# Attention value products of a hybrid decoder step: each product split over its queries onto the two column halves of the array

## The chip, the cores and the metric

The kernel runs on one core of one Trainium2 chip. The metric is the device time of one execution in microseconds (us); three runs of the kernel before gave 4284.92, 4284.16 and 4273.37 us, a median of 4284.16 us. Work is split over TensorE (matrix products; the profile shows its matmuls as PE and its weight loads as PEld), VectorE (DVE), ScalarE (ACT), GpSimd (POOL) and the queue that issues transfers (SP).

## The reference, cut to what matters

One decoder layer is computed for a prompt of 2048 tokens and for 8 samples. It has a combined input projection, two parallel head groups, an output projection, a SwiGLU network and an embedding gate. The two head groups of the prompt are:

- group A, a gated DeltaNet with 4 heads of width 128, which is a recurrence over chunks of tokens with a triangular system to solve in each chunk;
- group B, a dilated sliding-window attention with 8 heads of width 64, for three pairs of window and dilation, (128, 1), (512, 4) and (2048, 16). For each pair a block of 128 queries sees the keys of its own block and of the block before it, or, at dilation 16, where one block holds the whole strided sequence, of its own block alone.

The part that the change touches is the product of probabilities and values:

```python
s = einsum('bdnqhe,bdnkhe->bdnhqk', qb, kk) * (E ** -0.5) + b
pr = exp(s - max(s))
den = sum(pr)
o = einsum('bdnhqk,bdnkhe->bdnqhe', pr, vv) / den
```

## The kernel before

The program is a sequence of blocks that end one after the other: input projection, bias rows with the samples' recurrence, `delta_and_attention`, the merge with the samples' attention, output projection, gate and up, down projection, embedding gate. Only `delta_and_attention` (scratch names begin with `pb_`) is changed.

It loops over 16 chunks of 128 tokens. In one chunk it does the recurrence of group A for all four heads, and, laid between its steps, one unit of attention for each of the three dilations. A unit has 4 steps, a step is two heads, so that a chunk has 12 steps (`STEPS`). Step `j` goes through the engines so:

1. `score_pair` (L946) on TensorE: queries times keys, contraction over 64 rows, for steps `j` and `j + 1` in alternation on the upper and lower 64 rows of the array.
2. VectorE adds the bias (L1140) and takes the maximum (L1144).
3. ScalarE takes the exponential with its sum (L842).
4. `turn` (L961) on TensorE: transposes of the probabilities `e`, one per head and block of keys.
5. ScalarE copies them to `eT` (L834).
6. `values` (L972) on TensorE: for each of the two heads and each block of keys one product with `eT` as the stationary operand (128 keys by 128 queries) and 64 columns of `vtok` as the moving one, accumulated over the blocks of keys in the bank `OUTPUT`.
7. VectorE copies the bank to `uo` after each unit (L1150), and a transfer stores it.

The order on TensorE is written out by hand. `slot(j)` issues `unit_start` (L933, transposes of the values) where a unit begins, `score_pair(j)` for even `j`, `values(j - 2)` and `turn(j - 1)`; `chunk` puts slots 0 to 13 between the steps of group A. All operands here are f32. The profile shows each f32 matmul that is no transpose as two records, each with a weight load of its own, and a transpose as one. So `values` makes 8 pairs of weight load and matmul in the steps of the first two dilations, which have two blocks of keys, and 4 in those of the third: 8 x 8 + 4 x 4 = 80 in a chunk, 1280 in all.

Three forms of matmul stand in this stage. The attention's transposes and values and most of group A use the whole array, 128 rows by 128 columns; the scores use 64 rows by 128 columns; the triangular solve of group A (`in_halves`, L920) uses 64 rows by 64 columns, one product on the upper rows and the lower columns' counterpart on the lower rows, in alternation (`TOP` and `BOTTOM` are partitions 0 to 63 and 64 to 127). The profile prints the form as rows*columns.

Each engine takes its instructions in order, with semaphores between them. `values(j)` waits for `eT_copied` and, at the first step of a unit, for `o_copied`; its last matmul raises `pv_done`, for which ScalarE waits before it overwrites that `eT` buffer and VectorE before it copies the bank.

Of the kernel before, what the change touches and what calls it, by code (L numbers as in the profile page):

```python
# [552 lines left out]
def delta_and_attention(nc, t):  # L553
# [13 lines left out]
    with ExitStack() as ctx:  # L567
# [31 lines left out]
        vtok = [sbuf(f"pb_vtok{v}", [P, 2, AH * HD], F32) for v in range(len(DILS))]  # L599
# [4 lines left out]
        eT = sbuf("pb_eT", [P, 2, 4 * P], F32)  # L604
# [29 lines left out]
        def bank(n):  # L634
            return ps[:, n, :]

        TOP, BOTTOM = slice(0, HALF_CH), slice(HALF_CH, P)
# [13 lines left out]
        SCORES, TURNS, OUTPUT = 4, 6, 7  # L651
# [3 lines left out]
        def step_heads(j):  # L655

            first = j % 4 // 2 * 4 + j % 2
            return j // 4, (first, first + 2)
# [6 lines left out]
        def col(tile, h):  # L665
            return tile[:, h * P:(h + 1) * P]
# [233 lines left out]
        def _(pe):  # L900
# [4 lines left out]
            for c in range(NC):  # L905
                m = pe.transpose(ps[:, c // 8, c % 8 * 36:c % 8 * 36 + 36], logits[:, c * CH:(c + 1) * CH], ident[0:36, 0:36])
# [16 lines left out]
            def halves(par, j):  # L923

                return ((par, 1),) if j // 4 == 2 else ((1 - par, 0), (par, 1))
# [38 lines left out]
            def values(c, par, j):  # L964
                v, hs = step_heads(j)
                pe.wait_ge(eT_copied, c * STEPS + (j + 1))
                if j % 4 == 0:
                    pe.wait_ge(o_copied, c * UNITS + (v + 1))
                for n, h in enumerate(hs):
                    hh = slice(h * HD, (h + 1) * HD)  # L970
                    for unit, half in halves(par, j):
                        m = pe.matmul(bank(OUTPUT)[:, hh], col(eT[:, j % 2, :], 2 * n + half), vtok[v][:, unit, hh],  # L972
                                      start=j // 4 == 2 or half == 0, stop=half == 1)
                m.then_inc(pv_done, 1)

            def slot(c, par, j):
                if j % 4 == 0 and j < STEPS:
                    unit_start(c, par, j // 4)
                if j < STEPS and j % 2 == 0:
                    score_pair(c, par, j)  # L980
                if j >= 2:
                    values(c, par, j - 2)
                if 1 <= j <= STEPS:
                    turn(c, par, j - 1)
# [1859 lines left out]
```

## Time and profile before

| | |
|---|---|
| three runs | 4284.92, 4284.16, 4273.37 us; median 4284.16 us |
| profiled execution | 4278.54 us, of which the span from first to last instruction is 4276.8 us |
| mean granted TensorE clock | 0.905 of full speed |
| busy share of the span | PE 85%, PEld 81%, DVE 35%, ACT 27%, POOL 19% |
| stage of `delta_and_attention`, chunks only | from about 863 to 1812 us of the span |

The profile is one execution. A busy time counts the recorded duration of instructions; matmuls are pipelined and their recorded ends are modelled, so the distance from the start of one group of instructions to the start of the next says more of what they cost than their durations do. The granted clock is given as a share of full speed; its two levels are 1.2 and 2.4 GHz, 0.5 and 1.0 there.

### The profile page before, as it was taken

The numbers are of one execution on the slowest core, as the hardware profiler recorded it, in microseconds if no ns is written. First come the engines' busy times: TensorE is split into PE (matmuls) and PEld (weight loads), VectorE is DVE, ScalarE is ACT, GpSimd is POOL, SyncE is SP. The second block draws the span as 40 slices with busy tenths as digits, with TensorE's granted clock in tenths as the row PEclk, the third lists the DMA queues.
The fourth block names the chain that finished last, engine by engine and source line by source line (L and its number), as shares of the span: only waits on it lengthen the run. The fifth ranks groups of instructions, "written<-read, shape, count | busy, mean of one in ns | idle before, by whom it ended". The sixth has DMA issues, their size and how long they took to land. (4 is left out here: it accounts for less than half of the span.)

```text
span 4276.8 us, 58938 instructions
## 1 busy us (share of the span) xinstructions
PE 3653.6 (85%) x23914; PEld 3476.2 (81%) x23914; DVE 1489.8 (35%) x1892; ACT 1146.6 (27%) x2073; POOL 816.9 (19%) x428
## 2 busy tenths in 40 slices
PE   7998999598888888846784999999999699997786
PEld 6998998387777777745783999999999689887785
DVE  6451222255555555634386000000000133331443
ACT  4111211255544554510222101101011233331322
POOL 3001111111111111111310111110110344443222
PEclk9999999589889898975896999999999899998898
DMA  3223343422333233173343334211110545543310
GB/s 110 61 70 79 138 152 142 148 70 67 80 78 73 64 86 85 49 189 86 128 158 149 131 118 159 96 45 53 39 59 30 171 155 175 169 139 115 125 66 37
DMA packets 266019, 443.05 MB, mean 104 GB/s; under 512 B 55763, under 2 KB 209171, under 8 KB 250308
## 3 DMA queue, kind: packets, MB, share of 16 engines
q1 hardware_dynamic: 265868, 440.79, 32.5%
q8 instruction: 125, 2.05, 0.2%
q14 instruction: 26, 0.21, 0.0%
HBM read 300.13 MB, written 174.14 MB: 111 GB/s over the span
## 5 line engine op out<-in xcount | busy, mean ns | idle before, releaser
L78 PE MATMUL pd_prod<-pd_h_hi,pd_whi 128*128 128x412 f32 x1760 | 615.8, 350 | 34.1 <-DVE pd_h_lo L2258 34.1
L79 PE MATMUL pd_prod<-pd_h_hi,pd_wlo 128*128 128x412 f32 x1760 | 617.0, 351 | 0.0
L80 PE MATMUL pd_prod<-pd_h_lo,pd_whi 128*128 128x412 f32 x1760 | 616.9, 351 | 0.0
L78 PE MATMUL pa_proj<-pa_h_hi,pa_whi 128*128 128x412 f32 x1160 | 410.5, 354 | 53.1 <-DVE pa_h_lo L408 24.3
L79 PE MATMUL pa_proj<-pa_h_hi,pa_wlo 128*128 128x412 f32 x1160 | 409.5, 353 | 0.0
L80 PE MATMUL pa_proj<-pa_h_lo,pa_whi 128*128 128x412 f32 x1160 | 408.1, 352 | 0.0
L2267 DVE TENSOR_TENSOR pd_act<-pd_prod,pd_gate 128x412 f32<-128x412 f32 x110 | 64.5, 586 | 909.8 <-PE pd_prod L80 909.8
L78 PE MATMUL pe_prod<-pe_ahi,pe_whi 128*128 128x412 f32 x880 | 317.1, 360 | 72.2 <-POOL pe_wlo L2370 40.1
L78 PEld LDWEIGHTS pd_prod<-pd_h_hi,pd_whi 128*128 128x128 f32 x1760 | 331.9, 189 | 38.1 <-issue 29.8
L79 PEld LDWEIGHTS pd_prod<-pd_h_hi,pd_wlo 128*128 128x128 f32 x1760 | 332.1, 189 | 2.2
L80 PEld LDWEIGHTS pd_prod<-pd_h_lo,pd_whi 128*128 128x128 f32 x1760 | 331.7, 188 | 1.4
L2370 POOL TENSOR_TENSOR pe_wlo<-pe_w,pe_whi 128x1408 fp32r<-128x1408 f32 x80 | 261.3, 3286 | 309.5 <-ACT pe_whi L2381 309.1
L79 PE MATMUL pe_prod<-pe_ahi,pe_wlo 128*128 128x412 f32 x880 | 314.7, 358 | 0.0
L80 PE MATMUL pe_prod<-pe_alo,pe_whi 128*128 128x412 f32 x880 | 313.9, 357 | 0.0
L2194 POOL TENSOR_TENSOR pd_wlo<-pd_w,pd_whi 128x1024 fp32r<-128x1024 f32 x44 | 108.0, 2455 | 954.0 <-ACT pd_whi L2209 954.0
L78 PEld LDWEIGHTS pa_proj<-pa_h_hi,pa_whi 128*128 128x128 f32 x1160 | 220.7, 190 | 58.8 <-issue 35.6
L78 PEld LDWEIGHTS pe_prod<-pe_ahi,pe_whi 128*128 128x128 f32 x880 | 171.1, 194 | 79.0 <-POOL pe_wlo L2370 45.4
L79 PEld LDWEIGHTS pa_proj<-pa_h_hi,pa_wlo 128*128 128x128 f32 x1160 | 220.5, 190 | 1.9 <-issue 0.6
L80 PEld LDWEIGHTS pa_proj<-pa_h_lo,pa_whi 128*128 128x128 f32 x1160 | 220.3, 190 | 1.0
L842 ACT ACTIVATE pb_e<-pb_s,pb_uo 128x256 f32<-128x256 f32 (+1 forms) x384 | 176.7, 463 | 106.8 <-DVE pb_uo L1144 106.8
L972 PE MATMUL pb_ps<-pb_vtok,pb_eT 128*128 128x64 f32 x1280 | 193.1, 294 | 0.0
L972 PEld LDWEIGHTS pb_ps<-pb_vtok,pb_eT 128*128 128x128 f32 x1280 | 173.9, 207 | 22.3 <-issue 10.8
(353 smaller groups left out, 6291.4 us busy)
## 6 DMA issues: line engine op xcount, KB each, us to landing
pe_w<-in_w_down SPq DMA_DIRECT2D x80, 704.0 KB, 4.1
scratch_at<-pa_work SPq DMA_DIRECT2D x24, 1024.0 KB, 5.6
pb_qkv<-scratch_at SPq DMA_DIRECT2D x32, 768.0 KB, 7.3
scratch_a<-pd_act SPq DMA_DIRECT2D x22, 1030.0 KB, 5.3
pe_a<-scratch_a SPq DMA_DIRECT2D x5, 4532.0 KB, 21.3
pd_w<-in_w_gate_up SPq DMA_DIRECT2D x44, 512.0 KB, 5.9
out_new_cache_k<-in_cache_k SPq DMA_DIRECT2D x8, 2046.0 KB, 11.1
out_new_cache_v<-in_cache_v SPq DMA_DIRECT2D x8, 2046.0 KB, 16.3
```

The costliest lines, as they stand in the source:

```text
L78: pe.matmul(out, w_hi, a_hi, start=first, stop=False)
L79: pe.matmul(out, w_lo, a_hi, start=False, stop=False)
L80: return pe.matmul(out, w_hi, a_lo, start=False, stop=last)
L842: m = act.activation(keys_seen(e[:, j % 2, :], j)[:, n, :], keys_seen(s[:, j % 2, :], j)[:, n, :], ACT.Exp, bias=uo[v][:, nm:nm + 1], accu ...
L972: m = pe.matmul(bank(OUTPUT)[:, hh], col(eT[:, j % 2, :], 2 * n + half), vtok[v][:, unit, hh], start=j // 4 == 2 or half == 0, stop=half == 1)
L2194: pool.tensor_tensor(w_lo[:, par, :], w_raw[:, par, :], w_hi[:, par, :].bitcast(F32), ALU.subtract).then_inc(w_lo_done, 1)
L2267: dve.tensor_tensor(act_row[:, cols], prod_ps[:, b, 0:TB], gate[:, cols], ALU.mult).then_inc(acts_done, 1)
L2370: pool.tensor_tensor(w_lo[:, q, :], w_raw[:, q % 2, :], w_hi[:, q, :].bitcast(F32), ALU.subtract).then_inc(w_lo_done, 1)
```

## The change

In `values`, each product of 128 queries becomes two products of 64 queries each: the first half of the columns of `eT` gives partitions 0 to 63 of the output bank, the second half gives partitions 64 to 127. Both use the same moving operand. The products of the two halves are issued in alternation, for each head and block of keys. The flags `start` and `stop` stay as they were, and so does the one semaphore at the end.

```diff
                     for unit, half in halves(par, j):
-                        m = pe.matmul(bank(OUTPUT)[:, hh], col(eT[:, j % 2, :], 2 * n + half), vtok[v][:, unit, hh],
-                                      start=j // 4 == 2 or half == 0, stop=half == 1)
+                        for queries in (TOP, BOTTOM):
+                            m = pe.matmul(bank(OUTPUT)[queries, hh], col(eT[:, j % 2, :], 2 * n + half)[:, queries],
+                                          vtok[v][:, unit, hh], start=j // 4 == 2 or half == 0, stop=half == 1)
                 m.then_inc(pv_done, 1)
```

## Rows read from the trace of the kernel before

**Rows 1.** The page, busy time, share of the span and instructions of TensorE.
```profile
PE 3653.6 (85%) x23914; PEld 3476.2 (81%) x23914; DVE 1489.8 (35%) x1892; ACT 1146.6 (27%) x2073; POOL 816.9 (19%) x428
```

**Rows 2.** Busy time by stretch, with granted clock (PEclk): the stage and two chunks' lengths.
```profile
core 0: us, PE busy (x) PEld busy (x) DVE busy (x) ACT busy (x) POOL busy (x), PEclk, DMA share, GB/s
863.00:1812.00 949.00, 826.75 (x9422) 732.99 (x9420) 538.94 (x933) 482.93 (x1329) 159.17 (x172) 0.89 0.28 72
...
1043.00:1102.00 59.00, 50.18 (x531) 44.07 (x527) 29.84 (x51) 25.66 (x72) 9.06 (x10) 0.80 0.26 65
...
1751.00:1810.00 59.00, 50.47 (x621) 44.39 (x620) 36.91 (x64) 34.33 (x95) 9.22 (x10) 1.00 0.13 37
```

**Rows 3.** Groups of instructions by line in the stage, TensorE's matmuls.
```profile
L972 PE MATMUL pb_ps<-pb_vtok,pb_eT 128*128 128x64 f32 x1280 | 193.1, 294 | 0.0
```

**Rows 4.** Timeline of TensorE's matmuls: start, length, line, form, count [idle before].
```profile
1037.97 1.10 PE L972 MATMUL pb_ps<-pb_vtok,pb_eT 128*128 128x64 f32 x8
1038.91 0.60 PE L961 MATMUL pb_ps<-pb_const,pb_e 128*128 128x128 f32 x4
1039.35 1.06 PE L1022 MATMUL pb_ps<-pb_knT 128*128 128x128 f32 x8
1040.25 1.06 PE L1027 MATMUL pb_ps<-pb_qnT,pb_knT 128*128 128x128 f32 x8
1041.14 1.00 PE L972 MATMUL pb_ps<-pb_vtok,pb_eT 128*128 128x64 f32 x8
1041.98 0.61 PE L961 MATMUL pb_ps<-pb_const,pb_e 128*128 128x128 f32 x4
...
1049.77 0.68 PE L920 MATMUL pb_ps<-pb_XTh,pb_B 64*64 64x64 f32 x16
1050.38 1.10 PE L972 MATMUL pb_ps<-pb_vtok,pb_eT 128*128 128x64 f32 x8
1051.32 0.61 PE L961 MATMUL pb_ps<-pb_const,pb_e 128*128 128x128 f32 x4
1051.86 0.68 PE L920 MATMUL pb_ps<-pb_Z,pb_X 64*64 64x64 f32 x16
...
1053.72 1.95 PE L990 MATMUL pb_ps<-pb_one,pb_squares 128*128 128x2 f32 x16
1055.60 1.16 PE L946 MATMUL pb_ps<-pb_qkv 64*128 64x128 f32 x16
```

**Rows 5.** The same timeline, two of the value groups with one block of keys.
```profile
1021.69 0.66 PE L972 MATMUL pb_ps<-pb_vtok,pb_eT 128*128 128x64 f32 x4
1022.18 0.39 PE L961 MATMUL pb_ps<-pb_const,pb_e 128*128 128x128 f32 x2
...
1027.07 0.56 PE L972 MATMUL pb_ps<-pb_vtok,pb_eT 128*128 128x64 f32 x4
1027.46 0.39 PE L961 MATMUL pb_ps<-pb_const,pb_e 128*128 128x128 f32 x2
1028.83 1.10 PE L1092 MATMUL pb_ps<-pb_osq,pb_ones 128*128 128x512 f32 x2 [0.98 <-DVE pb_S L1228]
```

**Rows 6.** The same timeline, eight 64*64 records on one quarter of the array.
```profile
1014.57 0.65 PE L1041 MATMUL pb_ps<-pb_XT,pb_L 64*64 64x64 f32 x8 [0.53 <-issue]
1015.14 1.10 PE L972 MATMUL pb_ps<-pb_vtok,pb_eT 128*128 128x64 f32 x8
```

**Rows 7.** Timeline of weight loads in the samples' attention, 128 rows by 64 columns.
```profile
1958.17 0.54 PEld L1626 LDWEIGHTS pm_ps<-sa_ones,sa_masked 128*64 128x64 f32 x8 [0.22 <-issue]
```

**Rows 8.** Timeline of matmuls around the longest wait of a chunk.
```profile
1004.73 0.61 PE L961 MATMUL pb_ps<-pb_const,pb_e 128*128 128x128 f32 x4
1007.19 1.12 PE L920 MATMUL pb_ps<-pb_Z,pb_X 64*64 64x64 f32 x16 [1.85 <-issue]
```

**Rows 9.** Timeline of all engines, what VectorE does ahead of that wait.
```profile
1002.62 3.35 DVE L1155 RECIPROCAL pb_orr<-pb_orr 128x512 f32<-128x512 f32 x1
```

**Rows 10.** Who waited for whom in the stage: total us, times, longest us.
```profile
PE pb_ps L961 <- ACT pb_e L842: 15.8, 15, 1.2
```

**Rows 11.** Timeline of matmuls in a stretch of low granted clock.
```profile
998.37 1.97 PE L972 MATMUL pb_ps<-pb_vtok,pb_eT 128*128 128x64 f32 x8
1000.13 1.06 PE L961 MATMUL pb_ps<-pb_const,pb_e 128*128 128x128 f32 x4
```

## The prediction

> **What bounds the kernel now.** I read the busy shares first: TensorE leads with 85% and no other engine is over 35% [rows 1]. The change touches one stage, so I went to the stretches next. In the 949 us of chunks TensorE's matmuls are busy for 827 us, VectorE for 539 and ScalarE for 483, at a mean granted clock of 0.89 [rows 2]. Then the groups by line: the value products are 1280 records with no idle time in front of them [rows 3]. They never wait for their operands; they are simply TensorE's turn. Last, the timeline, from start to start. Behind a value group the transposes follow at once (1050.38, 1051.32, 1051.86), and in all the stage they wait for the exponentials for only 15.8 us in 15 places [rows 4, 10]. So a shorter value group mostly lets the whole order of TensorE move up, and the stage shortens with it; the later stages only shift. Only where a wait for another engine follows in the same chunk is the gain given back.
>
> **What a value group costs, and by what.** From start to start eight records take 0.94 us when the group before had another form, and 0.84 us when it had the same form (1037.97 to 1038.91; 1041.14 to 1041.98) [rows 4]. Without the change of form that is 0.105 to 0.11 us a record. Eight records with 128 moving columns take 0.90 us (1039.35 to 1040.25), 0.112 each, and sixteen with two moving columns take 1.88 us, 0.117 each [rows 4]. So the moving columns, 2 or 64 or 128, do not set the price. The load of 128 columns of weights does. Loads of 64 columns over 128 rows come in steps of about 0.057 us: eight in 0.54 us, of which the last record alone takes some 0.14 [rows 7]. Half the columns, half the time. The change makes twice as many loads of half the width, so everything depends on whether the two column halves work at the same time.
>
> **The nearest rows, one for each answer.** Sixteen 64*64 records in alternation on two quarters of the array take 0.61 us from their start to the start of a full-array group (1049.77 to 1050.38) [rows 4]. This is the price if the halves run together: two 64-column loads in the time of one. Eight 64*64 records on a single quarter take 0.57 us to the same point [rows 6]; sixteen would take that plus 8 x 0.058, 1.03 us. This is the price if they do not. The first row is nearer in what is asked, alternation between two halves with separate outputs in one bank, but its two products differ in rows as well as in columns. In the new group both halves read the same 128 partitions. No row shows that, and it is the open point of this forecast. I take the first price, because it is the row whose order of work is copied, and keep the second as the other end.
>
> The Trainium skill has rules on both sides. In "TensorE: Matmul & The Clock Gate", section "Measured speedup vs the span model", three packed column tiles with 512 moving columns run 2.38 times as fast; by that rule the two halves overlap at 2.38/3 of the ideal, an estimate of 0.51/0.79 + 0.10 = 0.74 us for sixteen records, and a sum of about -0.66 us a chunk, -11 us. The same page, section "The mechanism", says that a weight load overlaps with matmuls in flight only when the row group differs. By that rule the halves, which share all rows, run in turn, and the sum would be the slower one below. The rows do not separate the two, since their alternating forms all change rows.
>
> **The edit, term by term, if the halves run together.** A change of form costs time of its own: transposes of four take 0.44 us when the same form follows (1038.91 to 1039.35) and 0.54 when another does (1051.32 to 1051.86), so 0.10 us per change [rows 4]. The price of 0.61 includes the change at its end. The transposes behind a value group have the value group's form now; afterwards their first step is stretched, for which I allow 0.04 (a value group loses 0.10 in all when it is entered with a change [rows 4], part of it inside). Per chunk there are twelve groups:
> - Seven groups of eight records, already entered from another form (steps 0, 2 to 7): 0.94 becomes 0.61 + 0.04 = 0.65, so -0.29 each, -2.03.
> - Step 1, eight records behind products of the full form: 0.84 becomes 0.65 plus a new change of 0.10 at its entry, -0.09.
> - Step 8, four records behind scores: 0.49 now (1021.69 to 1022.18) [rows 5]. Eight records at the first price are 0.61 less 8 x 0.032 (the 0.61 less its change of 0.10, over 16), 0.36, and with the 0.04 it is 0.40: -0.09.
> - Steps 9 to 11, four records behind full-form products: 0.39 to 0.47 now, one of them 1027.07 to 1027.46 [rows 5]. They become 0.36 + 0.04 + 0.10 = 0.50, together +0.25.
>
> The sum is -1.96 us a chunk, -31 us over 16 chunks. What is given back: once a chunk TensorE stands for 1.85 us before L920, behind VectorE's reciprocal of 3.35 us [rows 8, 9]. The value group just ahead of it (step 5) is covered by that wait; what it saves makes the wait longer: +0.29 a chunk, +4.6 us. Step 10 stands ahead of the wait of 0.98 us for the state [rows 5], so its loss of 0.11 is free: -1.8 us. That leaves -28 us. I take a quarter off for smaller waits that now open up (the exponentials of rows 10, the copies of Z, the ends of chunks), which makes -22 us. At the low clock level eight value records take 1.76 us instead of 0.94 (998.37 to 1000.13) [rows 11], so in those stretches a group saves nearly double; with a mean clock of 0.89, about a fifth of the stage is at 1.2 GHz, worth up to 6 us more. I keep that as the lower end. Nothing moves in the other queues: no transfer, no wait and no semaphore is added, and the bank and buffers stay.
>
> **Result.** 4278.5 - 22 = 4256.5 us for an execution like the profiled one. It lies 5.6 us under the median of the runs, so against the median I forecast 4262 us, with its own range of 4240 to 4276 (the ends: all -31 and the low-clock 6 from the profiled run's level; a gain of only 8 us from the median).
>
> **Rival 1, the halves run in turn (slower).** The place is the value group itself, between one load and the next. Against it: the alternation at L920 runs pairwise. For it: no row shows two halves on the same rows. Sixteen records are then 1.03 us, with 0.04 behind: +0.13 for seven groups (0.91); step 1 1.03 + 0.14 - 0.84 = +0.33; step 8 0.57 + 0.04 - 0.49 = +0.12; steps 9 to 11 0.57 + 0.14 each against 0.39 to 0.47, +0.88. Together +2.24 a chunk, +36 us. Waits hide 0.13 at step 5 and 0.32 at step 10, 7 us in all: +29 us, 4313 us against the median. It decides as soon as sixteen records cost more than about 0.8 us from start to start: 0.61 plus 1.96/10, ten being eight groups and four of half the size, is where the twelve groups add up to zero.
>
> **Rival 2, the clock takes the gain back (no change).** One chunk's stretch has a granted clock of 0.80 and another 1.00 [rows 2], with the same program. Shorter groups make the waits a larger part. A mean clock lower by 0.025 in the stage is 0.05 x 949 = 47 us more at the low level; at double price for work and nothing for waits, that costs up to 23 us, the whole gain. For it: the wait in rows 8 grows, and behind it sixteen records of L920 last 1.12 us, where at full clock they last 0.68 [rows 4, 8]. Against it: the same matmuls stand in less time, so their density rises. Time: about 4282 us.
>
> That the change doesn't do what it says would be records at L972 that still read 128*128. The solve's output slices already give the 64*64 form, so I give this nothing of its own.
>
> **Chances.** Forecast 0.55, rival 1 0.27, rival 2 or a partial overlap that ends near zero 0.18. A measurement of this kernel can tell 0.3%, 13 us, from no change. Of the forecast's 0.55 some 0.07 falls inside 13 us: faster 0.49, within 0.22, slower 0.29. The range must reach into both signs: 4238 to 4318 us.
>
> **What the profile would show.** L972 with 2560 records of form 128*64. If right: sixteen of them in about 0.6 us from start to start; the transposes behind them 0.04 us longer; the stage some 22 us shorter, the wait before L920 some 0.3 us longer, its clock near 0.89. If sixteen take about 1.0 us, rival 1 holds. If they take 0.6 us and the stage is no shorter, the clock in the stage or the waits before L920, L961 and L997 say where it went. The forecast is wrong altogether if another stage changes its length.

## The result, and the profile after

The changed kernel took 4219.73 us (median of 6 runs, 4216.41 to 4228.01) against 4279.07 us for the kernel before in the same series: a ratio of 0.9868, 95% interval 0.9849 to 0.9886, 59 us faster. A second series gave 4228.73 against 4279.08 us, ratio 0.9884 (0.9862 to 0.9906), 50 us faster. The forecast was 4262 us, 22 us faster than the median of three runs, with a range of 4238 to 4318 us. The direction was right, the gain was more than twice as large, and the time lies 18 us below the range. (Of the 42 us between 4262 and 4219.73, 5 us come from the base: over six runs the median of the kernel before is 4279.07 us, not 4284.16.)

The page and the group of the value products, after. They answer to [rows 1, 3]; L973 is the line that was L972.

```profile
PE 3584.0 (85%) x25194; PEld 3384.1 (80%) x25194; DVE 1486.6 (35%) x1892; ACT 1145.6 (27%) x2073; POOL 817.1 (19%) x428
...
L973 PE MATMUL pb_ps<-pb_vtok,pb_eT 128*64 128x64 f32 x2560 | 124.7, 240 | 0.0
```

The records doubled to 2560 in the form 128*64, and the time in which at least one of them is under way fell from 193.1 to 124.7 us.

The timeline of TensorE's matmuls after, with the columns of [rows 4]:

```profile
1031.04 0.69 PE L973 MATMUL pb_ps<-pb_vtok,pb_eT 128*64 128x64 f32 x16
1031.66 0.66 PE L961 MATMUL pb_ps<-pb_const,pb_e 128*128 128x128 f32 x4
1032.15 1.06 PE L1023 MATMUL pb_ps<-pb_knT 128*128 128x128 f32 x8
1033.04 1.06 PE L1028 MATMUL pb_ps<-pb_qnT,pb_knT 128*128 128x128 f32 x8
1034.03 0.69 PE L973 MATMUL pb_ps<-pb_vtok,pb_eT 128*64 128x64 f32 x16
1034.64 0.66 PE L961 MATMUL pb_ps<-pb_const,pb_e 128*128 128x128 f32 x4
...
1039.32 0.69 PE L973 MATMUL pb_ps<-pb_vtok,pb_eT 128*64 128x64 f32 x16
1040.72 0.66 PE L961 MATMUL pb_ps<-pb_const,pb_e 128*128 128x128 f32 x4 [0.71 <-ACT pb_vtok L828]
```

Two rows of the kernel before, for the waiting transposes of step 2:

```profile
1046.53 1.10 PE L972 MATMUL pb_ps<-pb_vtok,pb_eT 128*128 128x64 f32 x8
1047.93 0.66 PE L961 MATMUL pb_ps<-pb_const,pb_e 128*128 128x128 f32 x4 [0.29 <-ACT pb_vtok L828]
```

And a group after in a stretch that is wholly at 1.2 GHz, 1.05 us from start to start, where [rows 11] show 1.76 us before:

```profile
1005.04 1.12 PE L973 MATMUL pb_ps<-pb_vtok,pb_eT 128*64 128x64 f32 x16
1006.09 1.12 PE L961 MATMUL pb_ps<-pb_const,pb_e 128*128 128x128 f32 x4
```

Sixteen records take 0.61 to 0.62 us from start to start, where eight took 0.94 or 0.84. The transposes behind them take 0.49 instead of 0.44 us. The products ahead of step 1 (1033.04 to 1034.03) take 0.99 instead of 0.89, the new change of form. At 1039.32 the gain is lost: the transposes now wait 0.71 us for ScalarE's copy of the values, where they waited 0.29 us before, and start 1.40 us behind the group's start in both kernels.

For groups of eight records, two rows of steps 9 and 10 (before 0.47 and 0.39 us):

```profile
1016.37 0.45 PE L973 MATMUL pb_ps<-pb_vtok,pb_eT 128*64 128x64 f32 x8
1016.76 0.44 PE L961 MATMUL pb_ps<-pb_const,pb_e 128*128 128x128 f32 x2
...
1020.10 0.45 PE L973 MATMUL pb_ps<-pb_vtok,pb_eT 128*64 128x64 f32 x8
1020.48 0.44 PE L961 MATMUL pb_ps<-pb_const,pb_e 128*128 128x128 f32 x2
```

The stretch of the chunks, first after, then before, busy times by engine and granted clock with the columns of [rows 2]:

```profile
859.00:1764.00 905.00, 764.66 (x10724) 647.80 (x10721) 537.59 (x934) 483.02 (x1334) 159.31 (x172) 0.93 0.30 77
```
```profile
861.00:1811.00 950.00, 828.75 (x9445) 734.70 (x9443) 538.61 (x933) 484.83 (x1334) 159.17 (x172) 0.89 0.29 73
```

The stage is 45 us shorter. The other 9 of the 54 us by which the spans differ lie in small pieces in stages that the change does not touch; in these stages, too, this execution of the kernel before had more time at 1.2 GHz, 609 us against 585. Why is not shown. The granted clock of the stage rose from 0.89 to 0.93. The trace records each stretch of the clock; summed over these two, TensorE was at 1.2 GHz for 201 us before and for 123 us after. That is the part the forecast does not have.

Waits of TensorE in the stage: total us, times, longest us. First three lines after, then two lines of before; the line before that goes with the second of them is in [rows 10]:

```profile
PE pb_ps L920 <- issue: 44.1, 29, 2.5
PE pb_ps L961 <- ACT pb_e L842: 16.8, 15, 1.2
...
PE pb_ps L961 <- ACT pb_vtok L828: 11.7, 16, 0.8
```
```profile
PE pb_ps L920 <- issue: 36.5, 26, 2.2
...
PE pb_ps L961 <- ACT pb_vtok L828: 4.9, 16, 0.4
```

These two waits grew by 14 us. In the full lists TensorE's waits in the stage add up to 113 us before and 134 us after.

### The profile page after: what moved, and what is told of

It reads as the page before. It is cut to its first block and busy times, and to the rows that moved or that the text cites. A ratio compares the mean times of both kernels' runs of the same rounds, so it can differ in the third digit from the quotient of the medians.

```text
span 4222.8 us, 61498 instructions
## 1 busy us (share of the span) xinstructions
PE 3584.0 (85%) x25194; PEld 3384.1 (80%) x25194; DVE 1486.6 (35%) x1892; ACT 1145.6 (27%) x2073; POOL 817.1 (19%) x428
## 5 line engine op out<-in xcount | busy, mean ns | idle before, releaser
L251 POOL TENSOR_TENSOR pa_wlo<-pa_w,pa_whi 128x1024 fp32r<-128x1024 f32 x29 | 85.6, 2953 | 546.8 <-ACT pa_whi L276 546.8
L2458 DVE TENSOR_TENSOR pe_alo<-pe_a,pe_ahi 128x824 fp32r<-128x824 f32 x55 | 67.1, 1294 | 346.9 <-ACT pe_ahi L2391 346.9
```

Source lines behind the costliest of these rows:

```text
L251: pool.tensor_tensor(w_lo[:, par, :], w_raw[:, par, :], w_hi[:, par, :].bitcast(F32), ALU.subtract).then_inc(w_lo_done, 1)
L2458: dve.tensor_tensor(a_lo[:, pair, :], a_raw[:, pair, :], a_hi[:, pair, :].bitcast(F32), ALU.subtract).then_inc(a_lo_done, 1)
```

## The experiments

Ten runs followed, nine altered kernels and the changed kernel once more. In the text and the table "low" is the time at 1.2 GHz in the stretch of the chunks, summed from the clock's record in the trace of the one profiled execution. The price is from the start of a value group of a step with two blocks of keys, entered from another form, to the start of the next group, the median of all such groups at full clock.

### First question: do the halves work at the same time, and is it the alternation?

**In turn.** All products of the upper queries first, then all of the lower.

```diff
-                for n, h in enumerate(hs):
-                    hh = slice(h * HD, (h + 1) * HD)
-                    for unit, half in halves(par, j):
-                        for queries in (TOP, BOTTOM):
+                for queries in (TOP, BOTTOM):
+                    for n, h in enumerate(hs):
+                        hh = slice(h * HD, (h + 1) * HD)
+                        for unit, half in halves(par, j):
```

> The changed kernel with the order of the value products altered: all products of the upper 64 queries first, then all of the lower 64, so that neighbours in the order lie on the same column half. Theory (the two halves run at the same time because neighbours alternate): the pairs are gone except at the one border, sixteen records take about 1.03 us from start to start against 0.615 with alternation, the sum per chunk is about +2.2 us against the kernel before, and the time is 25 to 50 us above it, about 4305 to 4330 us. Rival (the order does not matter, half-width loads are simply cheaper or the hardware reorders): sixteen records stay near 0.6 us and the time near 4220 us.

It took 4247.44 us against 4276.26 (ratio 0.9937, 0.9912 to 0.9962). TensorE's timeline, two value groups:

```profile
1020.24 0.46 PE L973 MATMUL pb_ps<-pb_vtok,pb_eT 128*64 128x64 f32 x8
1020.63 0.44 PE L961 MATMUL pb_ps<-pb_const,pb_e 128*128 128x128 f32 x2
...
1036.66 0.97 PE L973 MATMUL pb_ps<-pb_vtok,pb_eT 128*64 128x64 f32 x16
1037.56 0.65 PE L961 MATMUL pb_ps<-pb_const,pb_e 128*128 128x128 f32 x4
```

Sixteen records take 0.90 us, so alternation is worth 0.28 us a group. But both sides of the expectation were wrong. The group is cheaper than the 1.03 us of the theory and dearer than the 0.6 us of the rival, and eight records take 0.39 us, as if they alternated. And with groups as dear as this (0.90 and a new change of form behind, against 0.94) the kernel was still 29 us faster than before. Its low time is 109 us.

**One half.** The order of the run in turn, but both parts go to the same column half, where the second overwrites the first; half of the attention's output is left out. The line that makes the difference to the run in turn:

```diff
-                            m = pe.matmul(bank(OUTPUT)[queries, hh], col(eT[:, j % 2, :], 2 * n + half)[:, queries],
+                            m = pe.matmul(bank(OUTPUT)[TOP, hh], col(eT[:, j % 2, :], 2 * n + half)[:, queries],
```

> The order of the run in turn, but both parts of the queries go to the same column half (output partitions 0 to 63; the lower 64 queries overwrite the upper, and partitions 64 to 127 stay at the zeros set once). Nothing can overlap now. In the run in turn, eight records took 0.389 us and sixteen 0.896, and in its trace matmul starts in the middle of the sixteen lie only some 4 ns apart. Theory (TensorE starts products of the free half ahead of earlier ones for the busy half, if they are no more than about four records behind): without a second half eight records take about 0.57 us and sixteen about 1.03, the prices of the first forecast's slower rival; the streamed columns and the low-clock time (90 to 130 us in the stage) stay, and the time is 4258 to 4280 us, 15 to 30 us above the run in turn. Rival (half-width loads take 0.053 us each without any overlap): 0.389 and 0.896 us again, and a time near 4247 us.

4263.84 us against 4280.38 (ratio 0.9962, 0.9943 to 0.9981). The timeline:

```profile
1041.59 1.15 PE L973 MATMUL pb_ps<-pb_vtok,pb_eT 128*64 128x64 f32 x16
1042.66 0.66 PE L961 MATMUL pb_ps<-pb_const,pb_e 128*128 128x128 f32 x4
```
```profile
1026.69 0.68 PE L973 MATMUL pb_ps<-pb_vtok,pb_eT 128*64 128x64 f32 x8
1027.30 0.44 PE L961 MATMUL pb_ps<-pb_const,pb_e 128*128 128x128 f32 x2
```

Here sixteen take 1.07 us and eight 0.61. This is the price without overlap, a little above the expected 1.03 and 0.57. Alternation over two halves takes it to 0.62 and 0.38: sixteen alternating records cost what eight of a single half cost. So the halves overlap although they read the same 128 rows, and in the run in turn part of the work overlapped too.

**Per head.** The half changes per head, after four records.

```diff
-                    for unit, half in halves(par, j):
-                        for queries in (TOP, BOTTOM):
+                    for queries in (TOP, BOTTOM):
+                        for unit, half in halves(par, j):
```

> The changed kernel with the column half altered per head rather than per product: for each head first the upper 64 queries over its blocks of keys, then the lower 64, so that four records of one half stand before four of the other. Theory (the free half's work is started ahead over up to about four records): sixteen records take 0.62 to 0.65 us, as in full alternation, and the time is 4217 to 4230 us. Rival (only direct neighbours overlap): sixteen records take 0.85 us or more, and the time is 4240 us or more.

```profile
1038.95 0.73 PE L973 MATMUL pb_ps<-pb_vtok,pb_eT 128*64 128x64 f32 x16
1039.61 0.66 PE L961 MATMUL pb_ps<-pb_const,pb_e 128*128 128x128 f32 x4
```

The price is 0.66 us, close to the theory's 0.62 to 0.65 and far from the rival's 0.85. The time, 4239.21 us against 4280.38 (ratio 0.9909, 0.9886 to 0.9932), missed the theory's 4217 to 4230. Its profiled execution had a span of 4226.3 us, within 4 us of the changed kernel's, and is the fastest of the four, so the trace at hand does not show where the rest of the median went. The granted clock of its four executions was 0.913 to 0.916, against 0.916 to 0.919 in the six of the changed kernel's first series and 0.914 to 0.919 in its second, so the clock may have a part in it. That stays open.

### Second question: where do the other 30 us come from?

The run in turn pointed at the clock. Since the load of weights sets the price, the moving columns can be changed with little effect on it, on either kernel. Where columns are left out, the bank is also cleared once at the start.

**The kernel before, 128 moving columns.** Neighbouring heads' columns are overwritten, so the attention's output is another one.

```diff
-                    hh = slice(h * HD, (h + 1) * HD)
+                    first = min(h * HD, 6 * HD)
+                    hh = slice(first, first + 2 * HD)
```

> The kernel before with 128 moving columns instead of 64 in each value product (it overwrites neighbouring heads' columns, so its attention output is another one). By the rows of before, the price of a value record is set by its 128-column weight load, so eight records stay at 0.94 us. Only the number of columns that TensorE works on rises. Theory (the gain beyond the shorter groups came from a higher granted clock, and the clock follows how densely TensorE is used): the low-clock time in the stage falls from about 201 us toward the 123 us of the changed kernel, and the time by 15 to 35 us against before. Rival (the clock follows only the waits between groups, or the lower low-clock time was chance): low-clock time stays near 200 us and the time within 0.3% of before.

**The changed kernel, 2 moving columns.** 62 of 64 output columns are left out.

```diff
-                    hh = slice(h * HD, (h + 1) * HD)
+                    hh = slice(h * HD, h * HD + 2)
```

> The changed kernel with 2 moving columns instead of 64 in each value product (62 of 64 output columns of each head are left out, and the bank is cleared once at the start). Load-bound, so sixteen records should stay near 0.6 us or a little less. Theory (clock follows density of use): low-clock time in the stage rises from 123 us to 200 us or more, and the time by 20 to 50 us against the changed kernel, back toward 4250 us or above. Rival (clock follows waits or chance): low-clock time stays near 123 us and the time near 4220 us or a few us below.

**The changed kernel, 32 moving columns** (the same edit with `h * HD + HD // 2`; half the output columns are left out), and **the changed kernel again** beside it.

> The changed kernel with 32 moving columns in each half product (the other 32 columns of each head are left out, the bank is cleared once). All value products together then stream as many moving columns as in the kernel before, where each is 64 wide and there are half as many. It should separate the shorter groups from the clock. Theory (direct gain some 28 us of stage time, the rest by the clock, which follows the columns streamed): low-clock time in the stage goes back to about 200 us, sixteen records take about 0.59 us, and the time is 4238 to 4250 us. Rival (halves on alternating columns are themselves what keeps the clock up, whatever they stream): low-clock time stays near 123 us and the time at 4215 to 4222 us.

> The changed kernel once more, beside the next three on the same chip. Both theories: about 4220 us, low-clock time in the stage within 15 us of the 123 us seen.

**The kernel before, 2 moving columns** (62 of 64 output columns left out).

> The kernel before with 2 moving columns in each value product (the other 62 are left out, the bank is cleared once). Eight records stay near 0.9 us, because the load of weights sets the price. Theory: low-clock time rises from 201 us to 280 us or more, and the time to 4290 to 4320 us, although less is computed. Rival (the clock does not follow the columns, the earlier pair was chance): low-clock time near 200 us and a time of 4260 to 4278 us.

| kernel | moving columns | price us | low us | granted clock, all executions | time us | before beside it | ratio, 95% interval |
|---|---|---|---|---|---|---|---|
| before, narrow | 2 | 0.914 | 345 | 0.891 to 0.897 | 4300.35 | 4279.08 | 1.0056 (1.0036 to 1.0076) |
| before | 64 | 0.942 | 201 | 0.903 to 0.911 | | 4279.07 | |
| before, wide | 128 | 0.995 | 123 | 0.916 to 0.919 | 4256.26 | 4276.26 | 0.9951 (0.9931 to 0.9970) |
| changed, narrow | 2 | 0.564 | 280 | 0.897 to 0.902 | 4250.07 | 4276.26 | 0.9943 (0.9925 to 0.9960) |
| changed, 32 | 32 | 0.589 | 205 | 0.903 to 0.910 | 4250.57 | 4279.08 | 0.9937 (0.9915 to 0.9959) |
| changed | 64 | 0.616 | 123 | 0.916 to 0.919 | 4219.73 | 4279.07 | 0.9868 (0.9849 to 0.9886) |
| changed, again | 64 | 0.616 | 89 | 0.914 to 0.919 | 4228.73 | 4279.08 | 0.9884 (0.9862 to 0.9906) |
| in turn | 64 | 0.897 | 109 | 0.916 to 0.919 | 4247.44 | 4276.26 | 0.9937 (0.9912 to 0.9962) |
| one half | 64 | 1.076 | 109 | 0.918 to 0.920 | 4263.84 | 4280.38 | 0.9962 (0.9943 to 0.9981) |

The clock in the fifth column is the mean over the whole of each execution; for the kernel before it is that of the 31 executions beside these runs. The low time comes from one execution each, and the changed kernel's two, 123 and 89 us, show how far it scatters: the repeat missed its expectation of 15 us around 123.

One group each of before narrow and of before wide (where the value products stand in L973), for the prices with 2 and with 128 columns:

```profile
1043.47 1.05 PE L972 MATMUL pb_ps<-pb_vtok,pb_eT 128*128 128x2 f32 x8
1044.38 0.64 PE L961 MATMUL pb_ps<-pb_const,pb_e 128*128 128x128 f32 x4
```
```profile
1036.19 1.16 PE L973 MATMUL pb_ps<-pb_vtok,pb_eT 128*128 128x128 f32 x8
1037.19 0.60 PE L961 MATMUL pb_ps<-pb_const,pb_e 128*128 128x128 f32 x4
```

The stretches of the chunks; the third number from the end of each line is the granted clock. In this order: before narrow, before wide, changed narrow, changed with 32 columns, changed again, in turn.

```profile
854.00:1843.00 989.00, 882.97 (x9446) 788.89 (x9444) 540.49 (x935) 484.47 (x1334) 159.11 (x172) 0.83 0.28 70
```
```profile
861.00:1795.00 934.00, 807.92 (x9448) 712.99 (x9446) 538.91 (x935) 484.85 (x1335) 159.19 (x172) 0.93 0.29 74
```
```profile
865.00:1796.00 931.00, 813.28 (x10726) 703.32 (x10724) 540.92 (x934) 482.76 (x1334) 158.64 (x172) 0.85 0.30 75
```
```profile
866.00:1791.00 925.00, 792.45 (x10728) 679.37 (x10728) 539.26 (x934) 483.15 (x1335) 159.07 (x172) 0.89 0.30 75
```
```profile
865.00:1755.00 890.00, 751.30 (x10723) 637.41 (x10721) 538.32 (x934) 481.88 (x1334) 159.19 (x172) 0.95 0.31 78
```
```profile
864.00:1786.00 922.00, 794.83 (x10728) 680.19 (x10728) 538.40 (x934) 484.55 (x1335) 159.09 (x172) 0.94 0.30 75
```

VectorE and ScalarE are busy for the same time in every kernel, 538 to 541 and 482 to 485 us. Only TensorE differs. Three comparisons carry the answer.

Before narrow computes less than before at a slightly lower price, and is 21 us slower: the stage grows to 989 us at a clock of 0.83. Before wide does the reverse: 0.05 us dearer a group, 20 us faster, clock 0.93. These two show that the moving columns of the value products, changed alone, move the granted clock, and with it the time. They ran in different series, and the granted clocks of their executions do not overlap with those of the kernel before, so the clock's part is no chance of one series.

The changed kernel with 32 columns streams in all as many moving columns as the kernel before. Its clock is again 0.89 (205 us low), its groups are short, and it is 28.5 us faster. That is the gain of the short groups without the clock, some 5 us too much, because its prices are another 0.027 us under those of the changed kernel in 192 groups. So the shorter groups are worth some 23 us by this pair. (The time came out at the upper edge of the expected 4238 to 4250 us; the low time is as the theory said.)

The rest of 59 or 50 us, some 27 to 36 us, comes with the higher clock. The split is rough: by their intervals the 28.5 us can be 18 to 36, and the 59 us 49 to 65. The run in turn bears it out: its groups take 0.90 us with a new change of form behind them, which is no gain on 0.94, and it is 29 us faster. So does one half: its groups are dearer than before, 1.07 us, and it is 16.5 us faster.

There is a second way to the size. Among the executions of the unaltered kernel before, one took 4260.7 us from first to last instruction at a mean clock of 0.911 and another 4290.7 us at 0.903. That is about 758 and 832 us at 1.2 GHz, so 0.4 us of time went with each microsecond at the low level (a line through all 31 executions gives 0.39). For the 78 us less low time in the stage, 201 to 123, this gives an estimate of 31 us out of the 45 us by which the stage is shorter, and leaves 14 us for the shorter groups. So the clock's part is about 30 us by both ways, and that of the groups 14 to 23 us.

### Third question: is more to be had?

**Whole array in steps 9 to 11**, where four records were no dearer than the eight that replace them:

```diff
-                        for queries in (TOP, BOTTOM):
+                        for queries in ((TOP, BOTTOM) if j < 9 else (slice(0, P),)):
```

> The changed kernel with the column halves in steps 0 to 8 only; steps 9 to 11 (four records each, behind full-array products) use the whole array as before. By the sum of the terms these three steps lost about 0.25 us a chunk (0.39 to 0.47 became 0.38 plus 0.05 behind plus 0.09 at the entry), of which 0.11 hides in the wait for the state. Theory: 1 to 3 us faster than the changed kernel, about 4217 us, not separable from it by this measurement but visible in the distances from start to start. Rival (the clock decides more than such terms): a difference of 10 us or more in either direction, with low-clock time moved by 20 us or more.

4221.09 us, ratio 0.9874 (0.9853 to 0.9896). Its span was 4221.9 us, 0.9 us under that of the changed kernel, and the low time 126 us. That fits the expected 1 to 3 us and cannot be told from nothing.

**Wide norms.** The eight norm products of a chunk with 64 moving columns instead of 2, of which one is read (ScalarE's copy picks it at the new distance).

```diff
-                    m = pe.matmul(bank(3)[:, 2 * i:2 * i + 2], squares[:, (4 + i) % 8, :], ones[:, 0:2], start=True, stop=True)
+                    m = pe.matmul(bank(3)[:, HD * i:HD * (i + 1)], squares[:, (4 + i) % 8, :], ones[:, 0:HD], start=True, stop=True)
```

> The changed kernel with 64 instead of 2 moving columns of ones in the eight norm products (L991) of each chunk, which stand in the stretch of long weight loads ahead of frequent low clock; the first column of each is used as before, the result is the same. By the rows a record's price is set by its 128-column weight load, 0.117 us with 2 columns. Theory: the price stays, low-clock time in the stage falls below 123 us by 15 to 60 us, and the time by 4 to 15 us against the changed kernel run beside it. Rival (what is left of low clock belongs to the waits): no change, within 3 us.

4228.65 us beside 4228.73 for the changed kernel: no difference.

```profile
1042.22 2.00 PE L991 MATMUL pb_ps<-pb_one,pb_squares 128*128 128x64 f32 x16
1044.14 1.05 PE L946 MATMUL pb_ps<-pb_qkv 64*128 64x128 f32 x14
```

Sixteen records take 1.92 us instead of 1.88, and the low time of the stage is 130 us, against 123 and 89. So the expected fall by 15 us or more did not come, and in the total the rival was right.

But the columns did move the clock where they stand. The same 9 us of a chunk, from the start of the norm products on, first in the changed kernel and then with wide norms, with the columns of [rows 2] (clock 0.81 and 1.00):

```profile
1046.00:1055.00 9.00, 8.82 (x131) 7.79 (x126) 3.97 (x4) 2.62 (x10) 0.00 (x0) 0.81 0.01 3
```
```profile
1042.00:1051.00 9.00, 7.47 (x130) 6.50 (x125) 5.17 (x5) 3.05 (x10) 0.00 (x0) 1.00 0.01 3
```

The traces record each fall of the clock. In the changed kernel 10 of the stage's 29 falls came within 4 us of the start of the norm products, in its repeat 3 of 23, and in every other kernel 7 to 14. With wide norms there was none, and the low time in the first 9 us behind these starts was 0 us in all 15 chunks, against 34 and 10 us. From 9 to 30 us behind them it was 89 us instead of 68 and 55. What was gained behind the norm products was lost again later in the chunk, and why is not shown. So it is not the columns of the value products alone that move the clock; when wider products lower the total, these runs do not settle. Neither version beats the changed kernel.

## Why the prediction was wrong, step by step

- **What bounds.** Right. TensorE's order set the stage; VectorE and ScalarE were busy for the same time in every run, and what a value group saved moved the rest up, but for the waits above.
- **The price is set by the weight load.** Right, and now shown on the group itself: with 2, 64 and 128 columns eight records took 0.91, 0.94 and 1.00 us, so the columns add little. One reading on the way was off: the 1.88 us of sixteen records with two moving columns contain a change of form at their end. Without its 0.10 us a record costs 0.111 us, not 0.117, which is closer still to the other rows.
- **The two halves run together.** Right. 0.61 us was forecast for sixteen records, 0.616 measured, and neither the 1.03 us without overlap nor the 0.74 us of a partial one; 0.36 for eight, 0.38 measured; 0.04 for the stretched transposes, 0.05 measured; 0.10 for the new change of form, 0.10 measured.
- **The slower rival.** Its mechanism did not occur, but its prices were sound: 1.03 and 0.57 us forecast, 1.07 and 0.61 measured with one half.
- **What is given back.** Right in kind. The loss at step 5 was named; that step 2 would lose its gain to the copy of the values was not, and stood only in the quarter that was taken off. The direct gain was forecast as 22 us and came out at 14 to 23. The quarter was a guess, so how well its size fits is in part luck. At 1.2 GHz a group saved 0.71 us (1.76 to 1.05), a little more than double the 0.33 at full clock, where the prediction said nearly double.
- **The clock. This step failed.** The forecast took the mean clock of 0.89 as given and allowed the stretches at 1.2 GHz only to raise what the shorter groups save, by up to 6 us. It then gave the clock a rival of its own, but with the sign of a loss, because the waits would be a larger part. What the runs showed in its place: the same edit doubles the moving columns, since both halves take the same 64, and the low time fell from 201 us to 123 and 89 us. That was worth about 30 us, more than the shorter groups themselves. The rival's "against", that the work stands denser in less time, was nearer to it than the rival. But no rows of before held the number of moving columns against the clock, and it was not counted there that two products of half the width stream twice as many columns.

So the term that was mis-sized is the change of the clock: put at nothing, with a loss as its rival, and measured as the larger part of the gain. What is shown is that the moving columns of the value products move the clock; by what rule the clock answers to them stays open.

## What to carry to other kernels

Where a product of few moving columns is bound by its weight load, two products on the two column halves cost less, if they alternate: 0.62 against 0.94 us for a group of eight records here. Pay attention to the two changes of form, which took 0.05 and 0.10 us and cancelled the gain for groups of four records. Count what an edit does to the work that TensorE streams, not only to the length of its groups: in a stage at a mean clock of 0.89 the columns were worth more than the shorter groups. To separate the two, change the moving columns at a nearly unchanged price and look at the granted clock, of the stage and of each place in it: a total that stays the same can hide a fall in one place and a rise in another.

## What the runs showed of the hardware that was not expected

**TensorE starts matmuls of a free column half ahead of earlier ones.** In the run in turn the starts of sixteen records, from the first one on, are 0, 107, 165, 224, 282, 288, 340, 394, 399, 453, 457, 511, 569, 628, 686 and 744 ns. The steps of 58 ns are those of a single half. In the middle there are pairs 4 to 6 ns apart. The sixteen starts come apart into two runs of eight (0, 107, 165, 224, 282, 340, 399, 457 and, within 1 ns, the same from 288 on), each with the spacing of the run with one half: the second half begins when the fifth record of the first has just started, and runs beside the rest. Groups of four and four overlap from the start (0, 13, 107, 120, 166, 178, 224, 236 ns), and with one half alone there are no pairs at all (0, 107, 165, 224, 282, 340, 399, 457 ns). The records do not name the half; that a pair is one of each is inferred from these spacings. If so, "each engine takes its instructions in order", as it stands above, does not hold for TensorE's two column halves. The per-head order, four and four twice, cost 0.66 us against 0.61 for strict alternation and 0.90 for eight and eight.

The Trainium skill says in "TensorE: Matmul & The Clock Gate", section "The mechanism", that weight loads overlap with matmuls in flight only where the row group differs, and that matmuls keep their order in start and end. This kernel's two halves have the same rows and take 0.61 against 1.07 us, so the first does not hold here as the prediction read it, that the halves do not overlap at all, and the starts above speak against the second.

**Fewer computed columns made the kernel slower.** With 2 of 64 columns left in the value products the kernel before took 21 us more, and TensorE was at 1.2 GHz for 345 us of the stage instead of 201. In the same way the changed kernel lost 30 us by the same cut (4219.73 to 4250.07 us, in two series).

**Where the clock falls.** Of the 29 falls in the stage of the changed kernel, 10 came within 4 us of the start of the norm products, which have two moving columns, and 13 between 9 and 15 us behind it, each 0.6 to 2.2 us after the end of a wait of more than 1.5 us before L920.
